# Attention, samples and last projection of a two-layer streaming encoder put into one block, with first loads and splits moved ahead and three output tiles walked row by row

## What is computed

```python
def latent_attend(q_lat, q_rope, c, kr, w_uv, mask):
    s = (einsum('bqhk,bsk->bhqs', q_lat, c) + einsum('bqhr,bsr->bhqs', q_rope, kr)) * ATTN_SCALE
    p = softmax(where(mask, s, NEG_INF))
    o_lat = einsum('bhqs,bsk->bqhk', p, c)
    return einsum('bqhk,khv->bqhv', o_lat, w_uv)

# prompt: causal over chunks of 64, in blocks of 128 queries
# samples: each sequence attends to its 1024 cached rows (cache_ckv, cache_krope) and its 16 new rows
out = einsum('bte,ed->btd', o * silu(gate), w_out_b)      # 2048 -> 1024
y = layer_norm(ALPHA * x + out, ln_g, ln_b)
```

## Time and profile before

| | |
|---|---|
| median of 3 runs | 2098.81 us (2096.63 to 2101.6) |
| profiled execution, its own time | 2097.49 us |
| its span, first to last instruction | 2095.5 us, 31585 instructions |
| PE busy | 1945.0 us, 93% |
| DVE busy | 1116.9 us, 53% |
| ACT busy | 722.0 us, 34% |
| POOL busy | 468.1 us, 22% |
| mean granted clock of PE | 0.977 |
| moved by DMA | 158.73 MB, mean 76 GB/s |

### The profile page before, as it was taken

How to read it: one execution, slowest core, us unless ns; L and a number is a source line. 1 busy time by engine, 2 the same in 40 slices (tenths; PEclk the granted TensorE clock), 3 DMA queues, 4 the chain that set the end, 5 groups by cost and what they waited for, 6 DMA issues and landing times. The chain is left out here.

```text
span 2095.5 us, 31585 instructions
## 1 busy us (share of the span) xinstructions
PE 1945.0 (93%) x11755; PEld 1821.5 (87%) x11755; DVE 1116.9 (53%) x1948; ACT 722.0 (34%) x1231; POOL 468.1 (22%) x388
## 2 busy tenths in 40 slices
PE   7999999999779999999999999999999689968997
PEld 6999999999668899999888898988889589956886
DVE  4355545655567413322667667666666467634333
ACT  3323233332231212211445345354354367632010
POOL 0222122221212110000335345254354200001101
PEclk9999999999989999999999999999999889989999
DMA  5122122210174112232211111021021432346311
GB/s 160 41 74 63 31 61 63 73 57 18 54 256 126 63 45 75 74 104 89 73 39 52 49 42 49 23 64 49 30 61 42 110 74 72 112 144 197 115 66 40
DMA packets 194174, 158.73 MB, mean 76 GB/s; under 512 B 35920, under 2 KB 178768, under 8 KB 193840
## 3 DMA queue, kind: packets, MB, share of 16 engines
q1 hardware_dynamic: 188160, 136.26, 21.7%
q10 hardware_dynamic: 5184, 18.88, 2.5%
q0 software_dynamic: 752, 2.53, 0.3%
HBM read 115.78 MB, written 41.84 MB: 75 GB/s over the span
## 5 line engine op out<-in xcount | busy, mean ns | idle before, releaser
L114 PE MATMUL a_pj<-act_h,a_w_l 128*128 128x384 f32 x768 | 275.9, 359 | 7.5 <-DVE act_l L108 7.5
L1821 POOL TENSOR_SCALAR h_p<-h_p,h_rsum 128x128 f32<-128x128 f32 (+7 forms) x128 | 220.2, 1726 | 213.7 <-DVE h_rsum L2109 212.9
L115 PE MATMUL a_pj<-act_l,a_w_h 128*128 128x384 f32 x768 | 260.6, 339 | 0.0
L116 PE MATMUL a_pj<-act_h,a_w_h 128*128 128x384 f32 x768 | 260.4, 339 | 0.0
L114 PE MATMUL ps<-act_h,m_c_l 128*128 128x384 f32 x480 | 163.8, 341 | 4.4 <-DVE act_l L108 2.4
L115 PE MATMUL ps<-act_l,m_c_h 128*128 128x384 f32 x480 | 163.2, 340 | 0.0
L116 PE MATMUL ps<-act_h,m_c_h 128*128 128x384 f32 x480 | 163.1, 340 | 0.0
L114 PEld LDWEIGHTS a_pj<-act_h,a_w_l 128*128 128x128 f32 x768 | 144.9, 189 | 12.8 <-DVE act_l L108 8.2
L115 PEld LDWEIGHTS a_pj<-act_l,a_w_h 128*128 128x128 f32 x768 | 145.0, 189 | 3.4 <-issue 3.4
L116 PEld LDWEIGHTS a_pj<-act_h,a_w_h 128*128 128x128 f32 x768 | 144.6, 188 | 0.0
L114 PE MATMUL o_py<-o_w_h,o_g_l 128*128 128x512 f32 x288 | 115.3, 400 | 24.0 <-DVE o_w_l L108 20.2
(11 more groups left out here) (323 smaller groups left out, 4981.2 us busy)
## 6 DMA issues: line engine op xcount, KB each, us to landing
a_w_raw<-in_w_in_a SPq DMA_DIRECT2D x32, 512.0 KB, 4.1
m_c_raw<-in_w_in_b SPq DMA_DIRECT2D x20, 512.0 KB, 4.1
scratch_gate<-m_sg SPq DMA_DIRECT2D x16, 576.0 KB, 5.1
h_gate<-scratch_gate SPq DMA_DIRECT2D x64, 128.0 KB, 2.0
scratch_og<-h_gate SPq DMA_DIRECT2D x64, 128.0 KB, 1.7
o_w_raw<-in_w_out_b SPq DMA_DIRECT2D x16, 512.0 KB, 4.4
o_g_raw<-scratch_og SPq DMA_DIRECT2D x8, 1024.0 KB, 7.5
a_factors<-in_x SPq DMA_DIRECT2D x9, 512.0 KB, 4.8
```

The lines of the kernel that those rows point to most:

```text
L114: nc.tensor.matmul(out, ll, rh, start=first, stop=False)
L115: nc.tensor.matmul(out, lh, rl, start=False, stop=False)
L116: return nc.tensor.matmul(out, lh, rh, start=False, stop=last)
L1821: nc.gpsimd.tensor_scalar(weights_of(u), weights_of(u), rsum[:, u % PB], None, ALU.mult).then_inc(S["p_ready"], 1)
```

## The change

`heads`, `samples` and `output` now run in one block with `middle`; the barriers and the final waits of SP between them are gone, and buffers lie where earlier ones are dead. In detail:

- In the last pair, SP issues the sample queries and sequences 0 and 1 (5.5 MB) in `load_first`, after the queries' stores have landed and POOL has zeroed four pads, and ahead of the loop of stores and gate loads. POOL zeroes 8 pads behind unit 2.
- ACT and DVE split the first queries at unit 8. PE transposes the first keys between the values of groups 6 and 7, in banks 0 to 6; ACT and DVE split them there.
- SP issues the first group of inputs and rows 0 to 3 of `w_out_b` once the last scores are done, rows 4 to 6 once the cache of sequence 7 is split, rows 7 to 10 after the last `result`, rows 11 to 15 after the samples' stores have landed. A group of inputs now holds 4 heads by 3 tiles. The raw data lies in the place of the low part, which is written over it.
- PE walks tiles 0, 1 and 2 together, row by row, each with two banks; the multiplication by `w_uv` comes after row 3 in banks 6 and 7. Tiles 3 to 8 follow one by one. ACT splits the first group and rows 0 to 2 ahead of the last `result`; DVE gates the samples behind row 6.

The diff, cut to its core (`ahead` is 7, `later` 11, `first_tiles` 3; `phase_output` is removed; `samples_programs` keeps the loops of `phase_samples`):

```diff
@@ heads, SP
             if last:
-                row = d["cache_ckv"][0].rearrange("(j p) e -> p j e", p=P)
-                sp.dma_start(k.stage[...], row).then_inc(k.cache_loaded, 16)
+                sp.wait_ge(S["ql_stored"], 16 * PAIRS)
+                sp.wait_ge(S["qr_stored"], 16 * PAIRS)
+                k.samples.load_first(sp)
             else:
                 load_w(sp, pr + 1, False)
...
-        for s in og_stored:
-            sp.wait_ge(s, 64 * PAIRS)
@@ heads, POOL
+                if last and u == 2:
+                    pool.wait_ge(S["proj_out"], PAIRS * NP)
+                    k.samples.zero_first(pool)
@@ heads, PE
+            else:
+                k.samples.turn_first(pe)
             values(pr, NG - 1)
@@ heads, ACT (DVE alike, with ..._low, ahead of gated(pr, NG - 1))
+                if last and u == 8:
+                    k.samples.first_queries_high(act)
...
+            else:
+                k.samples.first_keys_high(act)
@@ samples
+    def load_first(sp):
+        sp.dma_start(ql_raw[:]..., d["scratch_ql"]...).then_inc(S["q_loaded"], 16)
+        sp.dma_start(qr_raw[0:RD]..., d["scratch_qr"]...).then_inc(S["q_loaded"], 16)
+        sp.wait_ge(S["zeroed"], 4)
+        load(sp, 0, 0)
+        load(sp, 1, 1)
...
+    def turn_first(pe):
+        pe.wait_ge(c_loaded[0], 32)
+        pe.wait_ge(kr_loaded[0], 64)
+        for j in range(NKT):
+            turn_keys(pe, j, j, j, 0)
@@ output, SP
+        sp.wait_ge(samples.S["s_done"], 2 * NSEQ)
+        for i in range(ahead):
+            if i == 0:
+                load_group(sp, 0)
+            if i == 4:
+                sp.wait_ge(samples.S["cl_ready"], NCP * NSEQ)
+                sp.wait_ge(samples.S["ql_ready"], NSEQ)
+                load_group(sp, 1)
+            load_row(sp, i)
+        sp.wait_ge(samples.S["o_out"], NSEQ)
+        for i in range(ahead, later):
...
+        samples.store_values(sp)
+        sp.wait_ge(samples.S["og_stored"], 64)
+        for i in range(later, nk):
+            load_row(sp, i)
@@ output, PE
+        for kt in range(nk):
+            pe.wait_ge(first_low, F0 + kt // GP + 1)
+            pe.wait_ge(wl_ready, W0 + kt + 1)
+            for t in range(first_tiles):
+                if kt == 0 and t == first_tiles - 1:
+                    pe.wait_ge(samples.S["o_out"], NSEQ)
+                columns(t, kt)
+            if kt == 3:
+                for j in range(4):
+                    samples.project_values(pe, j)
+        for t in range(first_tiles, NT):
+            if t >= 4:
+                pe.wait_ge(gl_ready, GL0 + t - first_tiles)
+                pe.wait_ge(sum_done, NT + max(t - 3, {4: 3, 5: 1, 6: 2, 7: 4}.get(t, 0)))
+            for kt in range(nk):
...
+                columns(t, kt)
@@ output, ACT (row_high) and DVE (the loop)
+    def row_high(act, i):
+        act.wait_ge(w_loaded[i if i < KD else KD + (i - KD) // 2], 32)
+        round_high(nc, w[i][0], w[i][2]).then_inc(wh_ready, 1)
...
+        for i in range(nk):
+            if i % GP == 0:
+                group_low(dve, i // GP)
+            row_low(dve, i)
+            if i == ahead - 1:
+                samples.gate_values(dve)
```

More of the change, by code:

```diff
@@ L2160, in body @@
                     split_low(dve, pr + 1, u - 5)
+                if last and u == 8:
+                    k.samples.first_queries_low(dve)
             gated(pr, NG - 2)
@@ new lines, in samples_programs @@
+    block = Programs()
+    kr_at = kept_at + 4 * (KEPT - 2 * SEQ)
+    tables_end = heads.tables_at + 8 * T
+    ends = nc.sbuf_top + 2 * KD * T * 4
+    early = Arena(nc, (kept_at, kr_at))
+    late = Arena(nc, (tables_end, ends), (kr_at, heads.weights_at))
+    spare = Arena(nc, (heads.weights_at, heads.stage_at))
+    ct_h, ct_l, kt_h, kt_l = [None] * 2, [None] * 2, [None] * 2, [None] * 2
+    block.first_rows_at = kept_at
+    ct_h[0], ct_l[0] = early.take("s_ct_h0", [2, KPAD], F32R), early.take("s_ct_l0", [2, KPAD], F32R)
@@ new lines, in samples_programs @@
+    olat = late.take("s_olat", [2, HEADS, P])
+    gate = Arena(nc, (heads.tables_at, tables_end)).take("s_gate", [HEADS, P])
+    mx = late.take("s_mx", [2, 1])
+    rsum = late.take("s_rsum", [2, 1])
+    bank = k.bank
+    uv = flat(ql_raw[:].rearrange("p h a t -> p h (a t)")).rearrange("p (a e) -> p a e", a=2)
+    names = ("q_loaded uv_loaded zeroed qh_ready ql_ready s_done masked max_done exp_done inv_done p_ready t_done t_high t_out "
+             "o_done o_out ch_ready cl_ready uv_done uv_out og_stored").split()
@@ new lines, in samples_programs, with _, turn_bank @@
+    block.zero_first = zero_first
+    @block.gpsimd
+    def _(pool):
+        pool.wait_ge(heads.S["pv_done"], PAIRS * NG)
+        pool.wait_ge(heads.S["o_out"], PAIRS * NG)
+        for x in (ct_h[1][:, :, KS:], ct_l[1][:, :, KS:], kt_h[1][:, KS:], kt_l[1][:, KS:], pt_h[:, KB], pt_l[:, KB]):
+            nc.gpsimd.memset(x.bitcast(F32), 0.0).then_inc(S["zeroed"], 1)
+    def turn_bank(pe, n, at):
+        if isinstance(n, int) and n <= NKT:
+            heads.bank_free(pe, at)
+        else:
+            pe.wait_ge(S["t_out"], n - 1)
+        return bank[:, at]
@@ L2678, in _ @@
                         heads.on_sync(sp)
+                        samples.on_sync(sp)
+                        output.on_sync(sp)
                     @block.gpsimd
@@ L2688, in _ @@
                         heads.on_tensor(pe)
+                        samples.on_tensor(pe)
+                        output.on_tensor(pe)
                     @block.scalar
@@ L2693, in _ @@
                         heads.on_scalar(act)
+                        samples.on_scalar(act)
+                        output.on_scalar(act)
                     @block.vector
```

1161 lines of the change are left out of this document (581 added, 580 removed).

## The result

The kernel after takes 2052.11 us (median of 4 runs, 2051.79 to 2052.9) against 2098.81 us (median of 3) for the kernel before beside it, a ratio of 0.9777 with a 95% interval of 0.9758 to 0.9796. A fourth run of the kernel before took 8983.04 us and is left out of median and ratio. The forecast was 2052 us. The profiled execution has a span of 2051.1 us, 44.4 us less than the 2095.5 of before.

A forecast was written before the change was run, and what follows sets the result against it. PE bounds the kernel, idle mainly at two block ends where it waits for transfers issued after a barrier. Gains of 33.2 + 12.5 = 45.7 us off the 2095.5 span, plus 2.0 us, give 2051.8, said as 2052; range 2042 to 2062.

The forecast's parts named there:

- Second place: Samples to output: PE goes straight from values into tiles, never waiting; 236.3 us shrink by 33.2 to 203.1 us.
- tight step, tile 4: Output: PE wants tile 4 at 1942.6, sum of tile 2 read at 1941.3; slack 1.3 us, 0 to 3 lost.
- rival D: Output walk does wait, tile 4 for its norm chain or a late row: 2 to 8 us, 2054 to 2060; chance 0.12.
- Rival F: Slower: PE granted 1.2 GHz in the output walk, 21.7 us more per tile, all nine 2247; chance 0.03.
- First place: Heads to samples: 21.3 + 1.3 - 0.3 - 1.0 - 6.8 - 2.0 = 12.5 us less.
- Boundary: Heads to samples: scores of sequence 0 start at 1656.3 instead of 1677.61, 21.3 us less.
- Clock at the first scores: Start of samples: first 3 us of scores ran at clock 0.50; dense work before them gives 1.3 us back.
- Pads and the query's split: Last pair of heads: POOL's pads delay unit 3 by 0.3 us; first query's split costs 1.0 us.
- Stall of gate 2: Last pair of heads: gate 2 lands at 1637.8, wanted at 1631.03; DVE stands 6.8 us, bounds 0 to 14.
- Slow clock behind the stall: Last pair of heads: a stall of this length drops PE's clock; 2.0 us lost.
- Rival B: Queue swallows the issues or drains sooner, gate 2 in time: 6.8 + 2.0 us more gained, 2043; chance 0.16.
- C: Backlog ahead of gate 2 longer, as far as 14 us and another slow clock stretch: 2057 to 2062; chance 0.16.

The follow-up runs named there:

- the four of the table: Profiles of after, after_again, gates_first and gates_first_again, listed together with 203.0 us from last result to the sum of tile 8.
- seq1_later: Kernel after with only the loads of sequence 1 (1.5 MB) moved behind gate 7; 2042.64 us.
- short_copy: Kernel after with the second copy of the rotary keys cut to one piece of eight in sequences 0 and 1 (448 KB not loaded); 2050.29 us.
- the second pair: Second profiles of the unedited kernels before and after (before_again, after_again); spans 2095.9 and 2048.0 us.
- gates_first: Kernel after with only the queries ahead of SP's stores and gate loads, sequence 0 behind gate 3, sequence 1 behind gate 7; 2042.02 us.
- before_again: Kernel before, no edit, profiled a second time; one run of 2097.66 us.
- after_again: Kernel after, no edit, profiled a second time; 2051.8 us.
- late_tile_by_tile: Kernel after with the output's first loads and splits only behind the last result, and tiles 0 to 2 walked one after the other; 2069.27 us.
- late_few_buffers: late_tile_by_tile, with a row issued only when the low part three rows before it is done (four from row 8 on); 2075.49 us.
- gates_first_again: gates_first, no edit, run a second time; 2043.6 us.

## Why the prediction was right

**Second place: right, term and reason.** It said 33.2 us less and 203.1 us of work. The stage takes 203.0 us in six profiles (the four of the table, seq1_later and short_copy), and 33.1 or 31.4 us less than in the two of before. The covers held: ACT ended the high parts of rows 0 to 2 at 1831.2, 4.8 us ahead of `result` at 1835.99.

```profile
1828.25 2.94 ACT L107 ACTIVATE o_w<-o_w_raw 128x1024 fp32r<-128x1024 f32 x3
1835.99 0.65 ACT L2347 COPY s_olat<-ps 128x256 f32<-128x256 f32 x2 [4.80 <-PE ps L120]
```

The tight step, tile 4, held as well. Moved by the 12.0 us between the two ends of the values, the forecast has norm 0 at 1910.8, the sum of tile 2 done at 1929.3 and PE there at 1930.6. (Its 1920.9 for the end of tile 2 does not follow from its own terms: 1847.7 + 72.6 are 1920.3, so that its slack should have been 0.7 us and not 1.3.) DVE:

```profile
1909.74 1.22 DVE L2711 SCALAR_TENSOR_TENSOR o_x<-o_x,ps 128x1024 f32<-128x1024 f32 x1
...
1927.25 1.21 DVE L2711 SCALAR_TENSOR_TENSOR o_x<-o_x,ps 128x1024 f32<-128x1024 f32 x1
```

Norm 0 started 1.1 us sooner and the sum was done at 1928.5, 0.8 us sooner. Tile 8 ended at 2038.9, five tiles of 21.74 us behind the start of tile 4, which was thus at 1930.2. So the slack was 1.7 us, and rival D did not come. Rival F did not either: every window in which PE walks the tiles stands at 1.00.

**First place: right in mechanism, a little low in sum.** It gave 12.5 us; the stages up to the last result give 22.1 + 1.9 - 8.4 = 15.6, and 17.2 in the second pair. Term by term:
- Boundary: 21.3 us forecast, 22.1 and 22.9 measured. The early loads, the missing barrier and the transposes moved ahead stand in it together; no run takes them apart.
- Clock at the first scores: 1.3 forecast, the samples are 1.9 and 2.1 us shorter. Of these, 1.5 and 2.2 us are there already at the first maximum on DVE, which starts 5.67 and 6.36 us behind the first score in the two profiles of before and 4.19 and 4.20 us behind it in the two of after.
- Pads and the query's split: 0.3 + 1.0 forecast, nothing measured. This was the mis-sized term. gates_first has both and needs 41.9 us from the query store to gate 6, as before_again does. Short operations in an engine's row of work are not on the path just because PE looks dense.
- Stall of gate 2: 6.8 forecast. DVE idled 6.14 us, and gate 2 came 5.9 us later behind the query store than before. The reckoning in bytes was good: counted from the query store, it had the store of group 0 at 23.7 us, and it was issued at 23.5 (at 23.1 to 25.1 in the six other profiles of the same order).
- Slow clock behind the stall: 2.0 forecast. From gate 2 to gate 6 are 22.06 us where before had 19.58 and gates_first 19.60, so 2.5 us more, of which the window at 0.50 above shows the place. In after_again it was 1.8.

**Outside the sum.** The end behind the sum of tile 8 became 0.6 to 0.7 us longer in every profile with the one block. I had counted on no change there, and its cause is open. The 3.6 us by which heads started late in the first profile belong to the execution. Forecast 45.7 us; the spans say 44.4 and 47.9. That the first hit the forecast almost to the digit is partly luck: in it, +3.1 us at the first place and -3.6 of the execution cancel.

**The rivals.** Rival B, the gate in time, did not come, but its price was right: 2043 forecast, and 2042.0, 2042.6 and 2043.6 us in the kernels whose gate is in time or nearly so. C would have needed a longer backlog; late_tile_by_tile and late_few_buffers show 7.96 and 7.95 us of wait with the same queue order, so the backlog itself varies by some 2 us.

By the Trainium skill, "DMA: Bandwidth & Descriptors", section Rules for kernel authors, a DMA is to be issued early and waited for late. The boundary, in which the early loads stand, became 22 us shorter; the rule says nothing on what is issued behind such a load on the same queue, and that cost 8 us here. Its section "Issuing engines are not separate DMA queues" says that transfers run on the same 16 DMA engines whichever engine has issued them, and no run here tests that. The trace shows only where the 128 KB of gate 2 waited: ahead of their issue, behind the issues of 5.5 MB and the store of group 0. Issued at 1638.35, they let DVE go on at 1640.53, 2.2 us later, against 2.0 us to landing in the median.

## What to carry to other kernels

Price a prefetch by what stands behind it in its queue: count the bytes ahead of the next small transfer, divide by the rate of a full window, and compare that with when the small one is needed. Put to the front of the queue only what is needed first; here the 1.5 MB of sequence 1 cost 9 of the 57 us that the change can bring. When a boundary between stages is removed, look first at what it held back: here, with the steps undone in this order, transfers issued before the engine gets there were 14 of 33 us and enough of them in flight 7, and the barrier alone at most 5 to 7. No run shows the early transfers with the barrier kept.

## What the runs showed of the hardware that I had not expected

- The same gap gives a different clock from one execution to the next: with PE busy 7.20 of 10 us in both, the granted clock was 1.00 in gates_first and 0.75 in gates_first_again, and the samples took 2.7 us less in the first. The cause is open. A saved stretch of low clock is a chance, not a certainty.
- SP was held by its own issues: single ones took 4.09, 5.41 and 2.33 us in the kernel after, where most take 0.35 to 0.73 us, and the DMA share was 0.97. Everything behind them in SP's program waits. What amount in flight brings this on no run shows.
- 448 KB in pieces of 256 bytes shortened the wait by 1.4 to 3.2 us, about what their bytes cost at the window's rate (1.9). I had kept as a bound that such pieces drain half as fast.
- The query store of the last pair, which has only work ahead of it that no edit touched, came 1608.78 to 1613.45 us into the span. Two profiles of each kernel were needed to see that 3.6 us of difference meant nothing.
